# Taking out the identity matmuls that stand ahead of the serial stretches of TensorE's program

## The reference

```
# first block
h = rms_norm(x, norm1_g);  proj = h @ w_in                    # 1024 x 3072
y = [diff_attention(4 heads, 2 maps each), moba_attention(8 heads)]
x = x + y @ w_out
x = x + hier_moe(rms_norm(x, norm2_g))                        # router, 32 experts, 2 per token
# second block
x = x + 0.5 * swiglu(rms_norm(x), w_gate, w_up, w_down)       # "ffn1"
z = rms_norm(x) @ w_in_2 + b_in_2                             # "mix"
x = x + (g0 * (attention(z) @ w_proj_attn) + g1 * (mlstm(z) @ w_proj_mlstm)) @ w_out_2
x = x + 0.5 * swiglu(rms_norm(x), ...)                        # "ffn2"
return rms_norm(x, final_norm)
```

## Time and profile before

| | |
|---|---|
| median of 3 runs | 1163.98 us (1163.68 to 1165.3) |
| profiled execution | 1168.42 us |
| its span | 1166.7 us |
| TensorE matmuls busy | 1095.2 us (94%) |
| weight loads busy | 828.4 us (71%) |
| DVE / ACT / POOL busy | 574.6 / 413.6 / 41.3 us |
| HBM read | 235.45 MB, 205 GB/s over the span |
| share of TensorE in the chain that ended last | 84% |
| mean granted clock of TensorE | 0.961 of full |

### The profile page before, as it was taken

The page is one execution under the profiler, slowest core; times in us unless marked ns, Lnnn a source line. Parts: engine busy times, 40 slices in busy tenths (PEclk is TensorE's granted clock), DMA queues, the critical chain, the costliest instruction groups (busy, mean ns, idle before and its releaser), DMA issues.

```text
span 1166.7 us, 13767 instructions
## 1 busy us (share of the span) xinstructions
PE 1095.2 (94%) x5569; PEld 828.4 (71%) x5569; DVE 574.6 (49%) x724; ACT 413.6 (35%) x518; POOL 41.3 (4%) x55
## 2 busy tenths in 40 slices
PE   5998899999999999999999999977899999999996
PEld 5866678454444447788888899855688887888885
DVE  4456836222222225444454547579765655444453
ACT  3424514211111114333333344364344334343332
POOL 1202000000000000000000000010000000000000
PEclk8979798999999999999999999877899999999999
DMA  7538028779999985655555355431055554655540
GB/s 233 196 134 305 4 108 356 328 317 393 419 410 414 418 312 175 206 171 183 188 180 180 127 181 181 145 108 37 2 198 181 182 163 142 192 176 186 203 144 36
DMA packets 102190, 239.49 MB, mean 205 GB/s; under 512 B 11670, under 2 KB 56802, under 8 KB 86786
## 3 DMA queue, kind: packets, MB, share of 16 engines
q1 hardware_dynamic: 99874, 229.05, 54.5%
q0 software_dynamic: 2272, 9.83, 2.5%
HBM read 235.45 MB, written 3.41 MB: 205 GB/s over the span
## 4 chain that ended last, share of the span: by engine, by line
PE 84%; DVE 8%; ACT 2%; issue 2%; DMA 1%; POOL 1%; SPq 1%; POOLq 0%; ACTq 0%; DVEq 0%
PE banks L921 18%; PE banks L923 18%; PE banks L922 18%; PE banks L1125 10%; PE banks L1140 5%; PE banks L1115 3%; PE banks L1106 3%; PE banks L928 2%; PE banks L995 1%; PE banks L1006 1%; PE banks L1240 1%; DMA bias_rows<-stage 1%; POOL head_stats L506 1%; DVE weights_lo L1475 1%; PE banks L1054 1%
## 5 line engine op out<-in xcount | busy, mean ns | idle before, releaser
L1475 DVE TENSOR_TENSOR weights_lo<-raw_weights,weights_hi 128x2048 fp32r<-128x2048 f32 x116 | 265.5, 2291 | 234.8 <-ACT weights_hi L613 234.8
L613 ACT ACTIVATE weights_hi<-raw_weights 128x2048 fp32r<-128x2048 f32 x116 | 221.5, 1912 | 203.9 <-PE banks L923 192.9
L921 PE MATMUL banks<-weights_hi,normed_T_hi 128*128 128x512 f32 (+1 forms) x624 | 247.7, 397 | 5.0 <-DVE stage L1784 3.1
L923 PE MATMUL banks<-weights_hi,normed_T_lo 128*128 128x512 f32 (+1 forms) x624 | 243.0, 389 | 0.0
L922 PE MATMUL banks<-weights_lo,normed_T_hi 128*128 128x512 f32 (+1 forms) x624 | 242.3, 388 | 0.0
L921 PEld LDWEIGHTS banks<-weights_hi,normed_T_hi 128*128 128x128 f32 x624 | 118.2, 189 | 37.0 <-issue 10.5
L923 PEld LDWEIGHTS banks<-weights_hi,normed_T_lo 128*128 128x128 f32 x624 | 117.9, 189 | 25.0
L922 PEld LDWEIGHTS banks<-weights_lo,normed_T_hi 128*128 128x128 f32 x624 | 118.1, 189 | 22.7
L1125 PE MATMUL banks<-expert_weights,stage 128*64 128x512 f32 x256 | 113.2, 595 | 0.0
L921 PE MATMUL banks<-weights_hi,ffn_hidden_T_hi 128*128 128x512 f32 x176 | 69.2, 393 | 3.0 <-DVE ffn_hidden_T_lo L1788 3.0
L923 PE MATMUL banks<-weights_hi,ffn_hidden_T_lo 128*128 128x512 f32 x176 | 69.2, 393 | 0.0
(11 more groups left out here) (305 smaller groups left out, 1591.6 us busy)
## 6 DMA issues: line engine op xcount, KB each, us to landing
raw_weights<-in_w_in SPq DMA_DIRECT2D x38, 1024.0 KB, 5.0
raw_weights<-in_ffn_w_gate SPq DMA_DIRECT2D x44, 512.0 KB, 3.9
raw_weights<-in_ffn_w_up SPq DMA_DIRECT2D x44, 512.0 KB, 4.9
raw_weights<-in_ffn_w_down SPq DMA_DIRECT2D x22, 1024.0 KB, 4.8
expert_weights<-in_w_gate SPq DMA_DIRECT2D x16, 1024.0 KB, 7.1
expert_weights<-in_w_up SPq DMA_DIRECT2D x16, 1024.0 KB, 9.3
expert_weights<-in_w_down SPq DMA_DIRECT2D x16, 1024.0 KB, 9.4
stage<-in_w_down SPq DMA_DIRECT2D x9, 1024.0 KB, 11.3
```

The lines of the kernel that those rows point to most:

```text
L613: ins = eng.activation(w_hi[:, slot, :], raw, ACT.Copy)
L921: eng.matmul(dst, x[0], w[0], start=first_one, stop=False)
L923: return eng.matmul(dst, x[1], w[0], start=False, stop=last_one)
L1475: ins = eng.tensor_tensor(w_lo[:, slot, :], raw, w_hi[:, slot, :], ALU.subtract)
```

## The change

The helper stay_warm and all calls of it are taken out; nothing else is changed. No wait is added or removed, and no other engine's list changes. The core of the diff (the places left out read alike: one call less, or the pair of numbers behind `True` less):

```
-            def stay_warm(n, bank):
-                for _ in range(n):
-                    eng.matmul(PS[:, bank, 0:P], ident[:, :], ident[:, :], start=True, stop=True)
...
-            def transpose8(u, src, ready, strided, idle=(0, 0)):
+            def transpose8(u, src, ready, strided):
                 for t in range(TILES):
-                    stay_warm(idle[t], 6)
                     eng.wait_ge(*ready(t))
...
-            transpose8(T_N1, tok, lambda t: (normed, TILES * N1 + t + 1), True, (12, 4))
+            transpose8(T_N1, tok, lambda t: (normed, TILES * N1 + t + 1), True)
...
-            stay_warm(14, 2)
...
-            stay_warm(12, 3)
             eng.wait_ge(assigned, 1)
```

More of the change, by code:

```diff
@@ L1038, in _ @@
                 blocks = [(a, kb) for a in maps for kb in range(t + 1)]
-                if t == 0:
-                    stay_warm(20, 7)
                 weight_transposes((0, t), blocks, lambda a: (weighted, 4 * t + a // 2 + 1) if a < 8
@@ L1074, in _ @@
             eng.wait_ge(gemm_used, 3)
-            stay_warm(10, 0)
             transpose8(T_N2, tok, lambda t: (normed, TILES * N2 + t + 1), True)
-            stay_warm(8, 2)
             copied8(T_N2)
@@ L1181, in _ @@
                 eng.wait_ge(tok_lo, t + 1)
-            stay_warm(4, 6)
             gather(0, 0)
-            stay_warm(4, 6)
             eng.wait_ge(ex_xT, 1)
             gather(0, 1)
-            stay_warm(4, 6)
             for u in range(2):
@@ L1284, in ffn @@
                 down_chunk(CHUNKS - 1, last + 3, False, True)
-            transpose8(T_F1, tok, lambda t: (normed, TILES * NF1 + t + 1), True, (22, 4))
-            stay_warm(9, 0)
+            transpose8(T_F1, tok, lambda t: (normed, TILES * NF1 + t + 1), True)
             ffn(0, T_F1)
-            transpose8(T_MIX, tok, lambda t: (normed, TILES * NMIX + t + 1), True, (13, 4))
-            stay_warm(11, 0)
+            transpose8(T_MIX, tok, lambda t: (normed, TILES * NMIX + t + 1), True)
             copied8(T_MIX)
@@ L1347, in _ @@
             eng.wait_ge(a_copied, 1)
-            stay_warm(13, 5)
             def gate_rows(t):
@@ L1417, in _ @@
             transpose8(T_MG, tok, lambda t: (merged, 3 + t), False)
-            stay_warm(12, 0)
             gemm_1024(G_OUT2, yT, T_MG, "w_out_2")
-            transpose8(T_F2, tok, lambda t: (normed, TILES * NF2 + t + 1), True, (13, 4))
+            transpose8(T_F2, tok, lambda t: (normed, TILES * NF2 + t + 1), True)
             ffn(1, T_F2)
```

## The result

| | before | changed |
|---|---|---|
| median of 8 runs, us | 1166.62 (1163.68 to 1169.72) | 1177.46 (1171.97 to 1180.09) |
| ratio, 95% interval | | 1.0085 (1.0063 to 1.0108) |
| profiled execution, us | 1168.42 | 1177.04 |
| its span, us | 1166.7 | 1175.3 |
| mean granted clock | 0.961 | 0.943 |

Slower by 0.85%, which is 9.9 us on 1166.6 (7.3 to 12.6); the medians are 10.8 us apart and the two profiled executions are 8.6 us apart. Two executions further down (1834 us in "Blocks fitted", 3256 us in its second part) lie far outside all others and are left out of their ratios.

A forecast was written before the change was run, and what follows sets the result against it. TensorE was taken to bound the kernel, its matmuls busy for 94% of the span. The terms summed to +14.1 us, 1182.5 from the profiled 1168.42; with the earlier median 4.4 us below that execution, the forecast was 1178, range 1169 to 1186.

The forecast's parts named there:

- Start, -3.0: Kernel start: first product begins 5.3 us sooner, low clock costs 2.3 us; 3.0 us faster (ends -3.9 and -1.5).
- the rival wait: At the start: weight pieces not split in time, so TensorE waits at piece 2 or 3; ratio 1.000, no chance given.
- First attention, +1.8: First attention from its 12 transposes on: clock still low, half of that time lost; 1.8 us slower (0.9 to 3.5).
- Routing and gather, +6.0: Transposes, router, positions and gathers at the low clock, less 0.7 us of block overhang; 6.0 us slower (3.5 to 8.5).
- ffn1 +2.0: ffn1: products open at the low clock, DVE's split hides the longer transposes; 2.0 us slower (1.3 to 2.6).
- mix +2.9: mix: tile 1's transposes cost 0.85 us and the products 2.0 at the low clock; 2.9 us slower (1.4 to 3.4).
- ffn2 +2.7: ffn2: tile 0's transposes cost 0.85 us, the products 2.0, less a little; 2.7 us slower (1.4 to 3.4).
- Second attention, 0: Second attention: products 0.4 to 0.9 us sooner, transposes up to twice as long; no net change (-0.9 to +2.0).
- Merge, +1.7: Products with w_out_2 after about 3 us idle: 1.7 us slower, though the clock may hold (0 to 2.6).
- The first: Whole kernel: clock holds in the gaps, only the blocks' overhang goes; 2.6 us faster, 1161.4 us; chance 5%.
- The second: Experts: if transfers set their pace, TensorE's later arrival is caught up and routing's 6.0 us goes; 1172 us; chance 15%.
- The third: Transposes don't bring the clock back, so it stays low longer where they open a stretch; +21.5 us, 1185.5 us; chance 15%.

The follow-up runs named there:

- Blocks fitted: Kernel before with the start's 12, 4 and 14 calls and the second attention's 13 out, the 12 ahead of the positions cut to 9: ratio 1.000.
- second part: Kernel before with the start's blocks and the 13 calls of the second attention out, all else as before: ratio 0.9965, median 1164.19 us.
- the norms: Kernel before without the calls of ffn1 (22, 4, 9), mix (13, 4, 11) and ffn2 (13, 4) alone: ratio 1.0051, median 1171.71 us.

## Why the prediction was right

The time fell on the forecast (1177.5 for 1178), in part by luck: the sum was 3.3 us over the difference of the medians (10.8), and the median of before, on which it was put, came out 2.6 us higher when more runs were taken. The rise was forecast at 14.1 us and is 9.9 by the ratio (7.3 to 12.6); the trace shows 8.6. Point by point:

- **The mechanism held.** Low clock at the openings, work there twice as long, no catching up behind.
- **When the clock fell.** One reading behind it was wrong. The clock was low from 17.3 on, but the 5.2 us without a matmul ran from 14.0 to 19.2, so it fell after 3.3 us of it. And the 5 us that the 22 calls of ffn1 cover are not longer than "either" idle stretch. Neither changed a term: at ffn1 the clock fell.
- **Start, -3.0.** -2.6 in the trace, -2.5 with the start alone. The low clock lasted 5.6 us instead of 4.5. Weight pieces were ready in time; the rival wait did not come.
- **First attention, +1.8.** +0.9 in both traces. I had TensorE low for 4 us; the clock was back after 3, with the 12 transposes, which count as work. 0.9 was the lower end. The runs with this block alone out say 3.0 (1.6 to 4.5), so the size is not settled.
- **Routing and gather, +6.0.** +4.9 and +6.5. The steps: transposes and router together +3.2 (forecast 3.4), positions +0.8, first gather +1.6. The second gather ran at full clock in one trace and low in the other, as the term had it by half.
- **ffn1 +2.0, mix +2.9, ffn2 +2.7.** 1.6, 2.8 and 2.0 in the trace, 6.7 together in the experiment; the cover by DVE's split ahead of ffn1 held.
- **Second attention, 0.** -0.3 across its own work, inside the ends (-0.7 with the clock before it).
- **Merge, +1.7.** 0 in the trace of the changed kernel, 1.6 in that with the merge alone. This is the term that was furthest off in the trace: a fall of the clock that came in one of two traces was put in at its full value.
- **The sum as a whole** was too high by 4.2 us for the ratio and by 5.5 for the trace, of which the merge is 1.7, the routing 1.1, the first attention 0.9, and ffn2 and the second attention 0.7 each. One reason runs through several of them. I let every opening pay the mean ramp of 4.1 us. In the changed kernel the transposes ahead had already brought the clock back in ffn1 (it was low again later for 3.4 us), the attention's ramp was 3 us, and the products of ffn2 were at the low clock for 3.5 us.
- **The parts, by the runs.** The ratios of the single edits add up to more than the whole: -4.9 for the start, 3.0 for the first attention, 6.1 for the routing, 6.0 for the norms and 2.7 for the merge make 12.9 us, where the change made 9.9. Each has an interval of 1.5 to 2.3 us on either side, so the two agree within the noise, and single terms are not known better than that.
- **Rivals.** The first (clock holds everywhere) is out by the traces of routing, mix and ffn2. The second is out by the experts' shift. The third is out by the blocks of transposes (ratio 0.9991) and by the clock's return during transposes alone at 458.7; so is the rule of the Trainium skill ("TensorE: Matmul & The Clock Gate", Part 4: PE-mode transpose) that transposes don't count as work for the clock, at least for these float32 ones. The other rule of that page, a ramp under 1% of the span, as the prediction applied it to the rise, came nearer than my sum: 0.85%, with an interval up to 1.08%.

## What to carry to other kernels

Filler matmuls ahead of a dense stage pay when they end as the wait ends; where they end later they delay real work that would have warmed the array itself, so each block wants its own look at when the next work was ready. Before a block is cut shorter, look at which clock it ran: the overhang may be that of the low clock and not of the number of calls, and the cut can cost more than the overhang did (12 calls cut to 9: 4 to 6 us by the runs). Price a place from both clock levels and the length of the ramp in the trace, and do not book a fall of the clock at its full value where the idle stretch is about as long as one over which the clock held.

## What the runs showed of the hardware

- Float32 transposes hold TensorE's clock like matmuls (ratio 0.9991 with all blocks made of them); matmuls that use 8 of the 128 rows do not (ratio 1.0347), though TensorE is busy without a gap.
- Float32 transposes alone bring the clock back: 0.50 until 458.6 and 1.00 from 458.7 in the changed kernel, with nothing else on TensorE since 455.44.
- After 2.9 us without a matmul the clock fell in one execution (940.0 to 943.3) and held in another (ahead of 945.11).
- Unchanged dense work behind an idle stretch of 1.5 us, at the end of ffn1, was at the low clock for 3.3 us in the kernel before and not at all in the one without the start's blocks, nor in two that keep them (routing alone, norms alone). One such place is worth about 1.6 us. The 29 runs of the kernel before on one chip lay between 1163.6 and 1171.6 us; that such places make this spread is likely and not shown. One trace therefore can't price a change of 1 to 2 us by its span; the shift at the place can.
